# Merge gates and mixer projections of a hybrid encoder block by a Strassen form

## What is computed

```
u = rms_norm(h, g_pre);  proj = u @ w_in
(c_b, c_c, c_x, c_z, q, k, v, r, lr_f, lr_b, m_a, m_b) = split(proj)
y_conv = c_b * conv3(c_c * c_x) * silu(c_z)
p_conv = y_conv @ w_out_c
o      = gla(q, k, v, forward) + gla(q, k, v, backward)     # chunked gated linear attention, 4 heads
y_gla  = rms_norm(o) * silu(r)
p_gla  = y_gla @ w_out_g
merged = sigmoid(m_a) * p_conv + sigmoid(m_b) * p_gla
out    = h + rms_norm(merged @ w_out, g_post)
```

## Time and profile before

| | us |
|---|---|
| median of 3 runs | 3067.92 |
| lowest, highest | 3067.82, 3123.69 |
| span of the profiled execution, slowest core | 3066.7 |
| spans of the 8 cores | 3059.2 to 3066.7 |
| mean granted TensorE clock of the cores | 0.995 to 0.997 of full speed |

### The profile page before, as it was taken

How to read it: one execution, slowest core, us unless ns; L and a number is a source line. 1 busy time by engine, 2 the same in 40 slices (tenths; PEclk the granted TensorE clock), 3 DMA queues, 4 the chain that set the end, 5 groups by cost and what they waited for, 6 DMA issues and landing times.

```text
span 3066.7 us, 55890 instructions; the slowest of 8 cores (3059.2 to 3066.7 us)
## 1 busy us (share of the span) xinstructions
PE 2983.7 (97%) x17724; PEld 1569.0 (51%) x17724; DVE 1626.7 (53%) x2546; ACT 1425.3 (46%) x2717; POOL 835.5 (27%) x1286
## 2 busy tenths in 40 slices
PE   5999999999999999999999999999999999999998
PEld 3555554444556655444456565444445555544443
DVE  5576661542666675163276667426237766723523
ACT  5767751321567763132256776213235686512211
POOL 4233333311422222132142222223123222312122
PEclk9999999999999999999999999999999999999999
DMA  7434546732411122262341112235233111133323
GB/s 181 98 77 102 105 117 146 215 112 76 154 61 44 44 66 90 76 216 84 93 147 44 44 48 66 96 114 186 76 109 117 51 46 44 58 105 99 121 78 122
DMA packets 136733, 301.28 MB, mean 98 GB/s; under 512 B 15088, under 2 KB 18032, under 8 KB 135936
## 3 DMA queue, kind: packets, MB, share of 16 engines
q1 hardware_dynamic: 122912, 272.34, 27.5%
q0 software_dynamic: 13536, 25.37, 5.5%
HBM read 265.80 MB, written 59.31 MB: 106 GB/s over the span
## 4 chain that ended last, share of the span: by engine, by line
PE 90%; issue 2%; DVE 2%; ACT 2%; DMA 2%; POOL 1%; SPq 0%; DVEq 0%; ACTq 0%; POOLq 0%
PE ps L471 87%; PE ps L476 3%; ACT L488 1%; ACT sb_AT L488 1%; DMA sb_W<-w_all 1%; DMA sb_onT<-x 0%; DVE sb_ycX L501 0%; POOL sb_stat L645 0%; DMA sb_ycT<-x 0%; DVE sb_AT L838 0%; DVE sb_CS L501 0%; POOL sb_stat L506 0%; DVE sb_ON L506 0%; DVE sb_TB L501 0%; DVE sb_ycT L497 0%
## 5 line engine op out<-in xcount | busy, mean ns | idle before, releaser
L471 PE MATMUL ps<-sb_uT,sb_W 128*128 128x512 bf16 (+2 forms) x8960 | 1885.3, 368 | 13.1 <-ACT sb_onT L488 7.6
L471 PEld LDWEIGHTS ps<-sb_uT,sb_W 128*128 128x128 bf16 (+1 forms) x8960 | 815.2, 98 | 932.5 <-issue 35.6
L488 ACT ACTIVATE sb_CS<-ps 128x512 f32<-128x512 f32 (+1 forms) x512 | 302.7, 596 | 902.2 <-PE ps L471 901.2
L501 DVE SCALAR_TENSOR_TENSOR sb_CS<-sb_CS,ps 128x512 f32<-128x512 f32 x256 | 176.1, 688 | 686.0 <-PE ps L471 682.9
L471 PE MATMUL ps<-sb_GR 128*128 128x512 bf16 (+2 forms) x1792 | 348.8, 318 | 2.6 <-ACT sb_AT L488 2.2
L497 POOL TENSOR_TENSOR sb_GR<-sb_CS 128x512 bf16<-128x512 f32 x128 | 162.0, 1266 | 693.6 <-DVE sb_CS L501 693.5
L501 DVE SCALAR_TENSOR_TENSOR sb_CS<-sb_CS,sb_convw 128x512 f32<-128x512 bf16 x256 | 221.1, 871 | 54.3 <-ACT sb_CS L488 41.0
L471 PE MATMUL ps<-sb_V,sb_uT 128*128 128x256 bf16 x2048 | 238.3, 274 | 0.0
L471 PEld LDWEIGHTS ps<-sb_GR 128*128 128x128 bf16 x1792 | 164.0, 98 | 134.1 <-issue 3.9
L471 PE MATMUL ps<-sb_onT,sb_W 128*128 128x512 bf16 x1024 | 232.0, 379 | 0.0
L471 PEld LDWEIGHTS ps<-sb_V,sb_uT 128*128 128x128 bf16 x2048 | 198.5, 98 | 27.9 <-issue 2.0
(11 more groups left out here) (122 smaller groups left out, 2979.2 us busy)
## 6 DMA issues: line engine op xcount, KB each, us to landing
sb_W<-wsc SPq DMA_DIRECT2D x496, 256.0 KB, 2.6
sb_onT<-x SPq DMA_DIRECT2D x50, 512.0 KB, 5.6
sb_W<-w_all POOLq DMA_DIRECT2D x80, 256.0 KB, 5.7
sb_GR<-x SPq DMA_DIRECT2D x40, 512.0 KB, 5.2
wsc<-sb_W SPq DMA_DIRECT2D x80, 256.0 KB, 5.1
y<-sb_GR SPq DMA_DIRECT2D x32, 512.0 KB, 2.9
sb_ycT<-x SPq DMA_DIRECT2D x32, 512.0 KB, 4.5
y<-sb_ycT SPq DMA_DIRECT2D x32, 512.0 KB, 3.1
```

The source lines that it names most:

```text
L471: S.add("pe", lambda e: e.matmul(out, lhsT=lhsT, rhs=rhs, start=start, stop=stop), r, w, cost=max(0.025, free_n(rhs) / 2400.0 + 0.0025) / ...
L488: S.add("act", lambda e: e.activation(out=out, in_=in_, func=func, **kw), r, w, table=TABLE.get(func), cost=0.17 + 0.82e-3 * free_n(in_) + ...
L501: S.add("dve", lambda e: e.scalar_tensor_tensor(out=out, in0=in0, scalar=scalar, in1=in1, op0=op0, op1=op1), r, w, cost=0.21 + 1.05e-3 * f ...
```

## The change

The four products of stage 6 are computed by Strassen's scheme in Winograd's form, over 2 x 2 blocks: two output blocks of 128 channels (of the pair p), two halves of the 1024 input channels, and two column halves of 512 tokens. Seven products of 4 matmuls each replace eight. A group is one kind and one pair: 4 kinds x 4 pairs = 16 groups for each half.

- **Operand sums** (`tsums`): T1 to T4 of `uT`, `ycT` and `onT` are made once per half, 24 bf16 sums of 1024 columns on DVE or POOL, in the chains TU, TY and TO. They lie in `GR` (u), `AT` (conv output) and the new `OS` (attention output; in batch 0's first half in `GR`).
- **Groups** (`group`): products 1, 6, 7 and 4 accumulate in one bank. Between them ACT copies the running sum out (`snap`), and DVE adds the products of other banks to these copies (`fold`). Products 5 and 3 share a second bank. Products 4 and 3 of a group are issued after products 1, 2, 5 and 6 of the next, and its product 7 after those.
- **Weight sums** (`prep`): the 32 half blocks of the four matrices are loaded as float32 (`w_pairs`), summed on ACT, POOL and DVE in 6 instructions each, and stored as bf16 (`wst`), spread over batch 0. The scheduler lets them wait while the engine is over `IDLE` = 2 us behind PE. 18 of them may alternate two output buffers (`ycX` and `OS`); from then on one is used.
- **Weight buffers**: `V` becomes part of `W2` (14 KB), which in stage 6 holds two blocks "a" (4 KB: four weight sums) and two "b" (3 KB: three). Stage 6 no longer uses `W1` for weights.
- **Order**: the output tiles of stage 7 of the first half come three conv units later, in batch 0 only near the end of the conv part; in batch 0 the output matrix is loaded after stage 6. Loads of residuals, of staged input and of the next batch's k wait for other items.

```diff
-    for d in range(8):
-        groups.append([("ma", d), ("oc", d), ("mb", d), ("og", d)])
...
-        return max(0.0, r - max(t, now), (t - now - BACKLOG) if e != "sp" else 0.0)
+        return max(0.0, r - max(t, now), (t - now - (BACKLOG if it.lim is None else it.lim)) if e != "sp" else 0.0)
...
-        w1 = WPool("W1", [Buf("W1", i * 2048, 2048) for i in range(3)])
-        w2 = WPool("W2", [Buf("W2", i * 2048, 2048) for i in range(5)])
-        wv = WPool("V", [Buf("V", 0, 4096)])
+        w1 = WPool("W1", "W1", {"c": [Buf("W1", i * 2048, 2048) for i in range(3)]}, 6)
+        w2 = WPool("W2", "W2", {"c": [Buf("W2", i * 2048, 2048) for i in range(5)],
+                                "a": [Buf("W2", 0, 4096), Buf("W2", 10 * KB, 4096)],
+                                "b": [Buf("W2", 4096, 3072), Buf("W2", 7168, 3072)]}, 14)
+        wv = WPool("V", "W2", {"v": [Buf("W2", 10 * KB, 4096)]}, 14)
...
+            for h in range(2):
+                c = 2 * h
+                put(chain, lambda c=c: step(two("T1", c), view(c, 1), view(c, 0), ALU.subtract), None, after[h])
+                put(chain, lambda c=c: step(two("T3", c), view(c + 4, 1), view(c, 1), ALU.subtract))
+                put(chain, lambda c=c: step(two("T2", c), two("T3", c), view(c, 0), ALU.add))
+                put(chain, lambda c=c: step(two("T4", c), view(c + 4, 0), two("T2", c), ALU.subtract), name if h else None)
...
+                def prod(bank, bk, h, sub, n, first):
+                    src = get(n)
+                    for c in range(4):
+                        w_ap, wkk = wbuf(h)(BF16, sub * 512 + c * 128, 128)
+                        s_ap, sk = src(c)
+                        mm(bank[:, 0:512], w_ap, s_ap, first and c == 0, c == 3, wkk + sk, bk, skip=not first)
...
+                def snap(i, s, bank, bk):
+                    q_ap, q_k = q[i][s](F32)
+                    act(q_ap, bank[:, 0:512], AF.Copy, bk, q_k)
+
+                def fold(i, s, bank, bk):
+                    q_ap, q_k = q[i][s](F32)
+                    tt("dve", q_ap, bank[:, 0:512], q_ap, ALU.add, bk + q_k, q_k)
...
+                def m6():
+                    bank, bk = G["gA", me]
+                    prod(bank, bk, ha, 0, "T2", False)
+                    snap(0, 1, bank, bk)
+                    rel(ha)
+                    fin(0, 0)
+
+                def m7(before):
+                    bank, bk = G["gA", me]
+                    prod(bank, bk, hb, 1, "T3", False)
+                    snap(1, 1, bank, bk)
+                    dbank, dbk = G["gD", me]
+                    fold(1, 1, dbank, dbk)
+                    if before:
+                        before["f01"]()
+
+                def m4():
+                    bank, bk = G["gA", me]
+                    prod(bank, bk, hb, 0, "T4", False)
...
+            before = None
+            for p in range(4):
+                for g in range(4):
+                    now = group(g, p)
+                    put("D2", lambda x=now, y=before: x["m1"](y), None, now["need"])
+                    for n in ("m2", "m5", "m6"):
+                        put("D2", now[n])
+                    if before:
+                        put("D2", before["m4"])
+                        put("D2", before["m3"], before["name"])
+                    put("D2", lambda x=now, y=before: x["m7"](y))
+                    before = now
+            put("D2", before["m4"])
+            put("D2", lambda x=before: (x["f11"](), x["m3"](), x["f01"]()), before["name"])
...
+            ops = [lambda: evac(o(2, 3)[0], f(0, 3)[0], f(0, 3)[1], o(2, 3)[1], engs=("act", "pool")),
+                   lambda: add(o(5), f(0), f(3), ALU.subtract),
+                   lambda: add(f(3), f(3), f(2), ALU.add),
+                   lambda: add(f(2), f(3), f(0), ALU.subtract),
+                   lambda: add(o(6), f(1), f(2), ALU.subtract),
+                   lambda: evac(o(0, 2)[0], f(2, 2)[0], f(2, 2)[1], o(0, 2)[1], engs=("act", "pool"))]
...
+            put("LP", load, ("pl", n), [("prepc", n - 2)] if n > 1 else [("r", 0, 0, 3)])
...
-            put("LW", lambda b=b: load_wo(b), None, [("O", b, 3, 0, 7)])
+            put("LW", lambda b=b: load_wo(b), None, [("O", b, 3, 0, 7)] if b else [("og", 0, 0, 7, 1), ("z", (0, 1, 2), 0)])
...
-                    if n % 4 == 0 and t7:
+                    if t7 and (n % 4 == 3 if b else 8 * j + n > 29 and (8 * j + n) % 3 == 0):
```

284 lines of the change are left out of this document (199 added, 85 removed).

## The result

| | before | after |
|---|---|---|
| median of 5 runs each, us | 3067.92 | 3030.86 (lowest 3027.93) |
| ratio after/before, 95% interval | | 0.9873 (0.9857 to 0.989) |
| span of the profiled execution, us | 3066.7 | 3029.3 |

The account below looks back on a forecast made before the run. PE was taken to bound stage 6, its time being the matmul count times 0.2158 us. Terms -110.5 - 1.5 + 14.6 + 1.8 + 2 + 3 + 6 = -84.6 us gave 2983 us, range 2957 to 3012.

Parts of the forecast that it names:

- Matmuls, -110.5: Stage 6, all eight: 512 fewer 512-column matmuls at 0.2158 us each take 110.5 us off.
- Gaps, +14.6: Both ends of each stage 6: PE waits 1.12 us for ACT's bank copy; 13 of 16 gaps stay unfilled, +14.6 us.
- Tail, +1.8: End of the last batch's second stage 6: the last merged tile comes late, leaving a 1.8 us gap before output tiles.
- First batch, +6: Batch 0: 32 weight preparations, 99 us of engine work in all, mostly fit beside other work and cost +6 us.
- Ready in time: Batch 0: all weight preparations are done at 347 us, before stage 6's first projection at 449.9.
- rival (c): First batch pays: ACT and DVE queues stand behind late loads, +32 to +64 us instead of 6, 3009 to 3041; chance 0.09.
- Operand sums, +2: Phase 1 and conv part: DVE has room for 24 sums, 16.5 us a stage; delayed phase 1 units cost +2 us.
- Keeps its 397 us: Sign: phase 1 of batches 1 to 3 keeps its 397 us within 1.
- Weights, +3: Stage 6 weight loads: hidden in steady state; 16 switches between block sizes cost 0.2 us each, +3 us.
- Conv part: Sign: the prediction is wrong if the conv part, where larger loads meet the next batch's, grows by more than some us.
- Late tiles, 0: Batch 0's conv part: output tiles starting 14 conv units later are covered by conv units, 0 us; a miss costs 8.
- (b): Steady stage 6: ACT's copies come late, costing 0.6 us in half or all of 128 groups, 3021 to 3060; chance 0.1.

Follow-up runs that it names:

- the run with 7 of 8: Kernel before with one of the eight accumulating matmuls of every stage 6 product left out, nothing else changed: ratio 0.9645, 2957 us.
- the version with other gaps: Changed kernel with products reordered in each stage 6's first and last groups, and the last group's first column half finished earlier: ratio 0.9800, 3008.67 us.
- other constants: Changed kernel with only the list scheduler's MARGIN 0.6 to 0.7 and TOL 0.02 to 0.1: ratio 0.9893; kernel before with the same constants: 0.9927, 3047.56 us.

## Why the prediction was wrong

**Matmuls, -110.5: right**, within 2 us, shown by the run with 7 of 8.

**Gaps, +14.6: right in kind and size.** 1.00 us instead of 1.12; the copy is waited for, as forecast. But the second halves don't have 2.2 us over 96.7, they have 5.5. Of these 0.9 are the next batch's transposes, which stood there before too (111.4 against 110.5). They do stand in the last gap, as supposed, but around them PE waits 0.95 us for weights and 1.57 us for a fold. PE's timeline there:

```profile
1526.97 1.02 PE L473 MATMUL ps<-sb_onT,sb_W 128*128 128x512 bf16 x4 [0.95 <-DMA sb_W<-wst]
1527.83 0.61 PE L478 MATMUL ps<-sb_ident,sb_ycX 128*128 128x128 bf16 x8
1528.83 1.02 PE L473 MATMUL ps<-sb_OS,sb_W 128*128 128x512 bf16 x4 [0.39 <-ACT sb_ON L490]
1531.42 1.57 PE L473 MATMUL ps<-sb_onT,sb_W 128*128 128x512 bf16 x4 [1.57 <-DVE sb_ON L499]
```

The transposes fill the gap on PE, and it shrinks to 0.39. That their copies on ACT and DVE are what the fold then waits behind is likely but not shown by a run. Filling a gap was worth less than its length. **Tail, +1.8: right** (a gap of 1.75), beside the 3 us of the scratch, which had no term.

**First batch, +6: wrong**, and this is the step that failed most; it failed in three ways.

*Readiness.* "Ready in time", at 347 us, took 6 to 10 us per preparation. From the first load (74.3 us) to the last (537.1) it is 14.9 us each, late in the phase 13.5, the last sums are stored at 561 us, and the first stage 6 keeps 9.7 of its 11.8 us of gain back. Being late had no price in the sum.

*Work.* The sum had 3.1 us each, 99 us in all, 45 of it on ACT, and took the row of a sum on DVE (0.42 us). The scheduler gave 78 of the 128 sums and 42 of the 64 copies to POOL, where a sum took 0.8 to 1.4 us on average against 0.5 to 0.7 on DVE (core 4; two of the groups):

```profile
L499 POOL TENSOR_TENSOR sb_OS<-sb_OS 128x256 f32<-128x256 f32 x37 | 33.9, 915 | 5.1 <-DVE sb_OS L499 1.0 <-POOL sb_OS L499 1.0 <-ACT sb_SM L490 0.2
L517 POOL CAST sb_OS<-sb_OS 128x768 bf16<-128x768 f32 x17 | 16.8, 988 | 15.7 <-DMA wst<-sb_OS 12.8 <-DMA sb_OS<-w_pairs 2.8
```

All groups of this kind add up to 154 us, 110 on POOL, 28 on DVE and 16 on ACT.

*Order and clock.* Most of the 18.6 us in phase 1 of batch 0 is neither, but waits that another order removes (15 us in the run without preparations) and the slow matmuls beside them. The sum had no term for it.

The whole is 18.6 + 9.7 + 3.7 (conv) = 32 us, the lower end of rival (c). Its mechanism, engines' queues standing behind landings, is there in part. The last row above has POOL waiting 15.6 us for transfers of the preparations, and one of PE's long waits goes back to a store (core 4):

```profile
307.06 0.58 POOL L530 DMA_DIRECT2D sb_W<-w_all  x1 [5.44 <-DMA wsc<-sb_W]
307.69 0.93 POOL L508 TENSOR_SCALAR sb_GR<-sb_TF,sb_dcol 128x256 bf16<-128x256 f32 x2
308.27 0.48 DVE L503 SCALAR_TENSOR_TENSOR sb_TF<-sb_TF,sb_dcol,ps 128x256 f32<-128x256 f32 x1 [4.65 <-POOL sb_GR L508]
...
309.50 0.27 PE L473 MATMUL ps<-sb_GR 128*128 128x128 bf16 x2 [3.53 <-DVE sb_GR L499]
```

But the longest wait of this stretch doesn't. PE's first releaser is POOL (20 to 463 us, core 4; in the kernel before it is 3.1 us, the longest 1.5), and behind its 4.92 us stand DVE and then ACT, which had loaded tables four times in 9 us:

```profile
PE ps L473 <- POOL sb_SB L508: 8.5, 5, 4.9
```

```profile
345.40 1.28 ACT L490 ACT_TABLE_LOAD   x1
...
347.40 0.48 DVE L503 SCALAR_TENSOR_TENSOR sb_onT<-ps,sb_glag,sb_onT 128x256 bf16<-128x256 bf16 x1 [3.38 <-ACT sb_onT L490]
...
348.45 0.48 POOL L508 TENSOR_SCALAR sb_SB<-sb_TB,sb_dcol 128x256 bf16<-128x256 f32 x1 [2.90 <-DVE sb_TB L503]
...
349.07 0.37 PE L473 MATMUL ps<-sb_SB,sb_GR 128*128 128x256 bf16 x1 [4.92 <-POOL sb_SB L508]
```

How much of the 32 us is (c)'s is open.

**Operand sums, +2: wrong as a term.** Phases 1 of batches 1 to 3 grew by 2.6, 3.8 and 5.7. ("Keeps its 397 us" takes a figure that no row has; the phase lasted 410 to 412 before.) The work was also undersized: 16.5 us a stage by a row of 687 ns, 26 us by the trace (core 4), as the first sums of `uT` take 1.44 us on DVE (20 of them, 0.69 to 0.93 for the others) and 31 of the 191 in the trace ran on POOL at 2.1 to 2.4 us.

Without the sums the growth is gone, but so it is, with all sums made, in the version with other gaps (409 to 410 us), and at other constants it comes back as 5 to 7. "Phase 1 keeps its 397 us within 1" assumed that the order outside the change stands still. In a drawn order there is no untouched code. How much is left for the sums in the best order is open.

**Weights, +3: not refuted**; in a second half PE waits 1.0 us for one load, in a steady first half for none. **Conv part**: +0.4 and +0.3 in batches 1 and 2, 0 in the last, +3.7 in batch 0. **Late tiles, 0**: nothing speaks against it, and early ones cost 12 us in the order that was drawn with them.

The clock was in no term at all. PE ran at 1.2 GHz for some 20 to 32 us per core before, and for 50 to 80 after, at 10 to 16 places of a core instead of 4 to 6; half of the difference is 18 us on core 0 and 24 on core 4, more than all gaps together (16 of 1.0). Between the two profiled cores (6 before, 4 after) it is 19 us, and that is most of why PE's busy time fell by 88 and not by 110 us.

The forecast's 85 us against 39 are then: some 18 in the stages 6 (the first one's late weights, the second halves), some 23 in the phases 1, 4 in the conv part of batch 0, 6 by the cores' wider spread, less 3 by the scratch. The measured time lies within what rivals (b) (3021 to 3060) and (c) (3009 to 3041) gave. For (b) that is chance: the steady pattern of a first half has its two forecast gaps and no other wait for ACT's copies. For (c) it is so in part, as said above.

## What to carry to other kernels

When a program's order is drawn by a scheduler, price a change together with a spread for the redrawing: change a constant of it without changing the work, and the difference (here 22 us of 3068, and 15 us in one phase) is the smallest effect that can be put down to the work. Look too for what the order itself makes an engine do, such as ACT's table loads. Compute for one-time preparations when the last is ready, with the cycle time of the whole chain through its shared buffers, its queues and the rule by which the scheduler places it, price each step on the engine that will get it, and give lateness a price. And count a wait on TensorE with what follows it: here a wait of 2.31 us was followed by 10 us at 1.2 GHz, which cost another 3 us or more in slow matmuls.

## What the runs showed of the hardware

The granted clock can fall to 1.2 GHz at a short wait: 1.3 us after one of 2.31 us between small matmuls, for 10.2 us; inside one of 3.54 us in front of transposes, for 20.5 us, in which five more waits of 1.5 to 2.3 us fell; inside one of 5.07 us in a stretch that was busy before, for 6.8 us. In the last, 8 matmuls of 512 columns went at 0.42 us each. The Trainium skill (TensorE: Matmul & The Clock Gate, "Wait — 56ns, not 53.3ns?") gives 426.7 ns for these at the low level and 215.7 at the high one, and the rows agree with both (0.42, and 0.2158 in the earlier trace rows).

A wait of the same length doesn't always bring it. In after on core 0 one of 2.23 us, ended at 241.6, was followed by 10.2 us at 1.2 GHz from 243.0 on, and one of 2.28 us, ended at 296.0, by none. What decides between the two was not settled.

A table load of ACT takes 1.28 us, and their number (106 to 126 in a run) moves with the order alone. The same sum of two 128x1024 bf16 operands took 0.69 to 1.44 us on DVE and 2.1 to 2.4 on POOL. With `dynamic_dma_scratch_size=4096` the program ended 3 us sooner after its last matmul.
